# A rewritten attention stage for one transformer trunk, with weight splits and the first map's scaling on POOL

## The chip, the cores and the metric

The kernel runs on one core of one Trainium2 chip. The metric is the device time of one execution in microseconds (us), as the median of the runs; lower is better. Engines: PE is TensorE (matmul), PEld its weight loads, DVE is VectorE, ACT is ScalarE, POOL is GpSimd, SP is SyncE, which here only starts DMAs.

## What is computed

Two residual layers over 512 tokens of width 1024, all in float32. Layer 0 mixes tokens by a gated MLP, layer 1 by differential attention; each is followed by a gated feed-forward block with a width-3 convolution, and each residual sum by a layer norm. The change touches the attention alone:

```
q, k, v = split(x @ w_qkv)           # 8 heads; q, k: 2 maps x 64; v: 128
logits  = q_j . k_j / 8 + bias(head, key - query)      # j = 0, 1
attn    = softmax(logits_0) - lam * softmax(logits_1)
o       = attn @ v                   # 512 x 128 per head
o       = o * rsqrt(mean(o^2) + eps) * subln_g * (1 - lambda_init)
out     = concat(o) @ w_out
```

## The kernel before

Each float32 product is made of three fast matmuls: an operand is split into hi (rounded, by an ACT copy) and lo (the rest, by a subtraction), and PE adds hi·hi, hi·lo and lo·hi in one PSUM bank (product, lines 988 to 994; every 128-wide product has these three lines, whatever the tensor). Tokens lie in four blocks t of 128.

The weights come in units of 128x2048 floats (1 MB). SP loads a unit into w_raw (two buffers), ACT makes w_hi (line 336 or 556), DVE makes w_lo (line 602), PE uses it. The semaphores are w_landed, w_hi_done, w_lo_done and w_used (a count of units that PE has left). Each engine has one instruction stream, written out by hand, and every wait blocks what is behind it on that engine.

The attention stage uses 12 units: U_BV to U_BV+3 for the values (4 heads in each pair of units, 512 columns wide), eight units U_QK+h with the queries and keys of head h, and then four units U_BO for the output product. On PE (lines 1235 to 1353) it runs so: tokens_first makes the values of heads 0 to 3 while the last rows are still being normalised; tokens_group (line 1045) makes those of heads 4 to 7 from U_BV+2 and U_BV+3; project (line 1240) makes q and k of heads 0 and 1 in banks 0 and 1; scores(0) makes the logits of head 0, block by block, in banks 2 (j=0) and 3 (j=1). Then head(h) runs for h = 0 to 6: turn_probs (line 1273) transposes the finished map of head h in 16 pieces through banks 5 and 6; scores (line 1258) makes the logits of head h+1; values (line 1289) multiplies the map by v into bank 7; project makes q and k of head h+2; mean_square (line 1303, matmul on line 1308) sums the squares into bank 4. After head 6 comes head 7 alone, woven with output units 0 and 1. Units 2 and 3 follow in outward (line 1079).

For one head and one block t the softmax is: DVE adds the bias and takes the maximum (scored, line 901, once per j, out of banks 2 and 3), ACT takes the exponential with its row sum (exps, line 525), DVE takes the reciprocals (909), scales the first map (911), makes the factor of the second (913) and mixes the two (917). DVE does scored(t+1) ahead of mixed(t). ACT and DVE split the transposed map (534, 931); ACT copies v_tok, splits each head's v (515, with 888 on DVE), squares the output of a head (541), and takes Ln and Exp for the root (547, 551), each behind a table load of its own. DVE writes the normalised o_t (939). In a head, ACT runs all of exps(h+1), the next unit's w_hi, and only then squares(h); DVE runs all of the softmax of h+1 and then w_lo of the next unit.

The bias tiles (256 KB for each block and head) are loaded by POOL (1471 to 1477) into bias_sb, each when DVE has read the one before. Apart from those, POOL does only the power for the layer norm's root (1465).

## Time and profile before

| | |
|---|---|
| three runs | 1385.53, 1384.03, 1385.91 us; median 1385.53 |
| profiled execution, first to last instruction | 1384.8 us, 15759 instructions |
| PE busy | 1310.7 us (95%) |
| DVE, ACT, POOL busy | 676.2, 460.4, 64.5 us (49%, 33%, 5%) |
| attention, from PE's last value matmul of heads 0 to 3 to its first of output unit 2 | 718.3 to 978.2 us |

Only the span of the profiled execution is given, not a separate time of its own; it lies 0.7 us under the median of the three runs. Matmuls are pipelined: a matmul's own duration is longer than the distance from one start to the next, and the distance is what counts. An entry "x8" or "x2" stands for so many instructions run together. "[1.78 <-ACT o_sq L541]" says that the engine sat idle for 1.78 us and that ACT's line 541 ended it.

### The profile page before, as it was taken

The numbers are of one execution on the slowest core, as the hardware profiler recorded it, in microseconds if no ns is written. First come the engines' busy times: TensorE is split into PE (matmuls) and PEld (weight loads), VectorE is DVE, ScalarE is ACT, GpSimd is POOL, SyncE is SP. The second block draws the span as 40 slices with busy tenths as digits, with TensorE's granted clock in tenths as the row PEclk, the third lists the DMA queues.
The fourth block names the chain that finished last, engine by engine and source line by source line (L and its number), as shares of the span: only waits on it lengthen the run. The fifth ranks groups of instructions, "written<-read, shape, count | busy, mean of one in ns | idle before, by whom it ended". The sixth has DMA issues, their size and how long they took to land.

```text
span 1384.8 us, 15759 instructions
## 1 busy us (share of the span) xinstructions
PE 1310.7 (95%) x6046; PEld 1070.9 (77%) x6046; DVE 676.2 (49%) x875; ACT 460.4 (33%) x549; POOL 64.5 (5%) x82
## 2 busy tenths in 40 slices
PE   7999999998999999999989889897999999999996
PEld 5788887888888888888868566665788888888884
DVE  2537664347433443323652677775664333443227
ACT  2422232213323232223222476765233223232220
POOL 3002000001000000000010100000010000000001
PEclk9999998999999999999999899998999999999998
DMA  7236931231322223223233232221222322223221
GB/s 287 91 92 143 237 107 61 91 122 62 120 92 91 91 91 111 102 91 121 87 98 95 79 99 76 81 87 61 73 80 92 119 93 91 91 91 110 103 91 61
DMA packets 96487, 140.54 MB, mean 101 GB/s; under 512 B 5120, under 2 KB 74840, under 8 KB 96192
## 3 DMA queue, kind: packets, MB, share of 16 engines
q1 hardware_dynamic: 88608, 119.55, 26.5%
q0 software_dynamic: 7840, 20.46, 5.3%
q8 instruction: 26, 0.43, 0.1%
q14 instruction: 13, 0.11, 0.0%
HBM read 137.85 MB, written 10.52 MB: 107 GB/s over the span
## 4 chain that ended last, share of the span: by engine, by line
PE 79%; DVE 10%; ACT 3%; DMA 3%; issue 3%; POOL 1%; DVEq 0%; POOLq 0%; SPq 0%; ACTq 0%
PE bank L990 27%; PE bank L994 25%; PE bank L993 25%; DMA w_raw<-in_a_w_in_dram 3%; DVE w_lo L602 2%; DVE x_tok L626 1%; ACT w_hi L336 1%; DVE r_stat L630 1%; POOL r_rs L1465 1%; DVE x_tok L646 1%; DVE prob L901 1%; PE bank L1308 1%; DVE xt_lo L608 1%; PE bank L1283 1%; DVE s_lo L616 1%
## 5 line engine op out<-in xcount | busy, mean ns | idle before, releaser
L990 PE MATMUL bank<-xt_hi,w_hi 128*128 128x512 f32 (+1 forms) x1024 | 391.2, 382 | 8.1 <-DVE xt_lo L608 6.6
L994 PE MATMUL bank<-xt_hi,w_lo 128*128 128x512 f32 (+1 forms) x1024 | 386.3, 377 | 0.0
L993 PE MATMUL bank<-xt_lo,w_hi 128*128 128x512 f32 (+1 forms) x1024 | 386.3, 377 | 0.0
L602 DVE TENSOR_TENSOR w_lo<-w_raw,w_hi 128x2048 fp32r<-128x2048 f32 x106 | 242.6, 2289 | 292.4 <-ACT w_hi L336 266.1
L990 PEld LDWEIGHTS bank<-xt_hi,w_hi 128*128 128x128 f32 x1024 | 194.1, 190 | 49.7 <-issue 10.3
L336 ACT CAST w_hi<-w_raw 128x2048 fp32r<-128x2048 f32 x60 | 114.5, 1909 | 323.9 <-PE bank L990 271.6
L993 PEld LDWEIGHTS bank<-xt_lo,w_hi 128*128 128x128 f32 x1024 | 194.1, 190 | 35.7 <-issue 1.4
L994 PEld LDWEIGHTS bank<-xt_hi,w_lo 128*128 128x128 f32 x1024 | 194.0, 189 | 35.4
L990 PE MATMUL bank<-w_hi,s_hi 128*128 128x512 f32 x544 | 214.9, 395 | 5.4 <-DVE s_lo L616 5.4
L993 PE MATMUL bank<-w_lo,s_hi 128*128 128x512 f32 x544 | 213.1, 392 | 0.0
L994 PE MATMUL bank<-w_hi,s_lo 128*128 128x512 f32 x544 | 212.9, 391 | 0.0
L990 PEld LDWEIGHTS bank<-w_hi,s_hi 128*128 128x128 f32 x544 | 103.1, 189 | 28.9 <-issue 7.8
L476 ACT CAST w_hi<-w_raw 128x2048 fp32r<-128x2048 f32 x42 | 80.0, 1906 | 134.3 <-PE bank L990 134.3
L993 PEld LDWEIGHTS bank<-w_lo,s_hi 128*128 128x128 f32 x544 | 103.2, 190 | 21.4 <-issue 0.2
L994 PEld LDWEIGHTS bank<-w_hi,s_lo 128*128 128x128 f32 x544 | 103.0, 189 | 21.6
L836 DVE SCALAR_TENSOR_TENSOR conv<-bank,conv_p,conv 128x511 f32<-128x511 f32 x44 | 33.0, 750 | 149.8 <-ACT conv L463 149.8
L463 ACT ACTIVATE conv<-bank,conv_p 128x512 f32<-128x512 f32 x44 | 34.3, 780 | 178.5 <-PE bank L994 178.5
L990 PE MATMUL bank<-w_hi,xt_hi 128*128 128x512 f32 x192 | 77.9, 406 | 13.3 <-DVE w_lo L602 10.9
L853 DVE TENSOR_TENSOR act<-conv,bank 128x512 f32 (+1 forms) x44 | 30.2, 687 | 98.8 <-PE bank L994 98.8
L994 PE MATMUL bank<-w_hi,xt_lo 128*128 128x512 f32 x192 | 76.5, 399 | 0.0
L993 PE MATMUL bank<-w_lo,xt_hi 128*128 128x512 f32 x192 | 76.5, 399 | 0.0
L1465 POOL TENSOR_TENSOR r_rs<-r_ve,neg_half 128x1 f32<-128x1 f32 x16 | 27.3, 1706 | 1011.4 <-DVE r_ve L634 1011.4
(132 smaller groups left out, 1134.4 us busy)
## 6 DMA issues: line engine op xcount, KB each, us to landing
w_raw<-in_f_w_in_dram SPq DMA_DIRECT2D x44, 1024.0 KB, 5.1
w_raw<-in_f_w_down_dram SPq DMA_DIRECT2D x22, 1024.0 KB, 4.8
w_raw<-in_a_w_in_dram SPq DMA_DIRECT2D x16, 1024.0 KB, 5.6
bias_by_query_key<-bias_by_distance POOLq DMA_DIRECT2D x4, 2048.0 KB, 35.9
w_raw<-in_a_w_out_dram SPq DMA_DIRECT2D x8, 1024.0 KB, 4.9
bias_sb<-bias_by_query_key POOLq DMA_DIRECT2D x32, 256.0 KB, 2.9
w_raw<-in_b_w_qkv_dram SPq DMA_DIRECT2D x16, 512.0 KB, 4.9
w_raw<-in_b_w_qkv_dram SPq DMA_DIRECT2D x4, 1024.0 KB, 5.1
```

The costliest lines, as they stand in the source:

```text
L336: act_e.copy(w_hi[:, u % 2, :], w_raw[:, u % 2, :]).then_inc(w_hi_done, 1)
L463: act_e.activation(conv[:, j, :], bank[j][:, :], ACT.Identity, bias=conv_col(l, NCP - 1, off + j), scale=conv_col(l, 1, off + j)).then_inc ...
L476: act_e.copy(w_hi[:, u % 2, :], w_raw[:, u % 2, :]).then_inc(w_hi_done, 1)
L602: dve.tensor_tensor(w_lo[:, u % 2, :], w_raw[:, u % 2, :], w_hi[:, u % 2, :], ALU.subtract).then_inc(w_lo_done, 1)
L608: ins = dve.tensor_tensor(xt_lo[:, 4 * h:4 * h + 4, t * P:t * P + P], bank[2 * t + h][:, :].rearrange("p (k n) -> p k n", n=P), xt_hi[:, 4 ...
L616: dve.tensor_tensor(s_lo[:, k % 2, :, :], src[:, bass.ds(i * (2 * step) + 2 * k, 2), :] if step else src[:, 2 * k:2 * k + 2, :], s_hi[:, k ...
L836: dve.scalar_tensor_tensor(out=conv[:, j, 1:S], in0=bank[j][:, 0:S - 1], scalar=conv_p[:, l, bass.ds(off + j, 1)], in1=conv[:, j, 1:S], op ...
L853: dve.tensor_tensor(dst, conv[:, j, :], bank[2 + j][:, :], ALU.mult).then_inc(act_done, 1)
L990: ins = pe.matmul(o, a_hi, b_hi, start=start, stop=False)
L993: pe.matmul(o, a_hi, b_lo, start=False, stop=False)
L994: return pe.matmul(o, a_lo, b_hi, start=False, stop=stop)
L1465: pool.tensor_tensor(r_rs[:, t:t + 1], r_ve[:, t:t + 1], neg_half[:, 0:1], ALU.pow).then_inc(rstd_done, 1)
```

## The change

The stage keeps its arithmetic and gets a new order on every engine, with all head loops written out.

- Units: the values of heads 4 and 5 (U_V45) and of heads 6 and 7 (U_V67) are units of their own, 256 columns wide, and value_pair multiplies them. U_V45 is woven between the blocks of scores(0), U_V67 between the blocks of the last scores. Project(1) follows scores(0).
- The values are split once, straight out of PSUM (values_hi, values_lo), for all heads; the per-head copies go.
- Within a head PE runs project(h+2) in pieces of 2, 3, 3 and 3, 5 rows of k between transposes, scores and values. mean_square sits behind 9 of the matmuls of project(h+2, 1).
- ACT makes the next unit's w_hi between the transposed pieces, squares(h) ahead of exps(h+1, 3), and loads the Ln table before it waits for the mean square.
- POOL makes w_lo of U_QK0 to U_BO+2 (11 units, four subtractions of 512 columns each), and scales the first map (shares) in place of DVE's line 911. DVE's mixed(t) waits for POOL's shares(t).
- SP loads the bias tiles, in line with the weight units. bias_sb moves to the place of ln_bc.
- Head 7, output units 0 and 1: cut into token blocks and halves. U_BO+2 is split into the place of the values of heads 0 to 3.

```diff
+    U_QK0 = U_BV + 2
+    U_V45 = U_BV + 3
+    U_QK1 = U_BV + 4
+    U_V67 = U_QK1 + H - 1
+    U_BO = U_V67 + 1
...
+        def hi_of(u):
+            if u == U_BO + 2:
+                return val_hi[:, 0:H // 2, :, :].rearrange("p h t n -> p (h t n)")
+            return w_hi[:, u % 2, :]
...
+                if n == 2:
+                    sp.wait_ge(sc_done, 2 * TB * H)
...
+            def load_bias(h):
+                for t in range(TB):
+                    if h:
+                        sp.wait_ge(sc_done, 2 * TB * (h - 1) + 2 * t + 2)
+                    sp.dma_start(bias_sb[:, t, :], bias_dram[h, t * P:t * P + P, :]).then_inc(bias_landed[t], 16)
+
+            load_qk(0)
+            load_unit(U_V45, cols(b_w_qkv[0], 2 * D + NB, 2 * P), dst=raw(U_V45, 2 * P))
+            sp.wait_ge(bias_made, 1)
+            sp.wait_ge(rows_ready, TB * 2)
+            load_bias(0)
+            load_qk(1)
+            load_qk(2)
+            for h in range(1, H - 2):
+                load_bias(h)
+                load_qk(h + 2)
+            load_bias(H - 2)
+            load_unit(U_V67, cols(b_w_qkv[0], 2 * D + NB + 2 * P, 2 * P), dst=raw(U_V67, 2 * P))
+            load_bias(H - 1)
...
+                if u == U_BO + 2:
+                    act_e.wait_ge(pv_mm, H // 2)
...
+                    act_e.wait_ge(ms_mm, h)
...
+            def root(h):
+
+                act_e.preload_act_table_set("natural_log")
+                act_e.wait_ge(ms_mm, h + 1)
...
+                act_e.activation(o_rs[:, :], bank[4][:, :], ACT.Ln, bias=eps_col[:, 0:1]).then_inc(ln_done, 1)
+                act_e.wait_ge(ln_done, h + 1)
+                act_e.activation(o_rs[:, :], o_rs[:, :], ACT.Exp, scale=-0.5).then_inc(rs_o_done, 1)
...
+            weights(U_QK0)
+            for n in range(TB):
+                values_hi(n)
+            weights(U_V45)
+            query_key(0, 0)
+            query_key(0, 1)
+            weights(U_QK1)
+            exps(0, 0)
+            values_hi(TB)
+            exps(0, 1)
+            exps(0, 2)
+            values_hi(TB + 1)
+            exps(0, 3)
+            weights(U_QK1 + 1)
+            query_key(1, 0)
+            query_key(1, 1)
+            for h in range(H - 2):
+                probs_hi(h, 0)
+                probs_hi(h, 1)
+                weights(U_QK1 + h + 2)
+                probs_hi(h, 2)
+                probs_hi(h, 3)
+                exps(h + 1, 0)
+                exps(h + 1, 1)
+                query_key(h + 2, 0)
+                exps(h + 1, 2)
+                squares(h)
+                exps(h + 1, 3)
+                root(h)
+                query_key(h + 2, 1)
+            h = H - 2
+            probs_hi(h, 0)
+            probs_hi(h, 1)
+            weights(U_BO)
+            probs_hi(h, 2)
+            probs_hi(h, 3)
+            exps(h + 1, 0)
+            values_hi(TB + 2)
+            exps(h + 1, 1)
             stationary(o_t, None, 0, o_done, 2)
+            exps(h + 1, 2)
+            values_hi(TB + 3)
+            exps(h + 1, 3)
             weights(U_BO + 1)
+            squares(h)
             stationary(o_t, None, 1, o_done, 4)
-            head(H - 1)
-            outward(o_t, U_BO, U_F[1] - U_BO, o_done, H, begun=True)
+            root(h)
+            h = H - 1
+            probs_hi(h, 0)
+            probs_hi(h, 1)
+            probs_hi(h, 2)
+            probs_hi(h, 3)
+            weights(U_BO + 2)
+            squares(h)
+            root(h)
+            stationary(o_t, U_BO + 1, 2, o_done, 6)
+            weights(U_BO + 3)
+            stationary(o_t, U_BO + 2, 3, o_done, H)
+            weights(U_F[1])
             enter(3, U_F[1])
             ffn(1)
...
+            def weighed(h, t):
+
                 n = TB * h + t
-                dve.wait_ge(exp_done, 2 * n + 2 + (0 if i is None else i * (4 * TB)))
+                dve.wait_ge(exp_done, 2 * n + 2)
                 dve.reciprocal(rsum[:, t, :], psums[:, t, :]).then_inc(rs_done, 1)
-                dve.wait_ge(rs_done, n + 1 + dyn4)
-                dve.tensor_scalar(prob[:, t, 0, :], prob[:, t, 0, :], rsum[:, t, 0:1], None, ALU.mult
-                                  ).then_inc(p0_done, 1)
+                dve.wait_ge(rs_done, n + 1)
                 dve.tensor_scalar(c1[:, t:t + 1], rsum[:, t, 1:2], neg_lam[:, 0:1], None, ALU.mult
                                   ).then_inc(c1_done, 1)
-                dve.wait_ge(p0_done, n + 1 + dyn4)
-                dve.wait_ge(c1_done, n + 1 + dyn4)
+
+            def mixed(h, t):
+
+                n = TB * h + t
+                dve.wait_ge(p0_done, n + 1)
+                dve.wait_ge(c1_done, n + 1)
                 dve.scalar_tensor_tensor(out=prob[:, t, 0, :], in0=prob[:, t, 1, :], scalar=c1[:, t:t + 1],
                                          in1=prob[:, t, 0, :], op0=ALU.mult, op1=ALU.add).then_inc(mixp_done, 1)
...
+            for n in range(TB):
+                values_lo(n)
+            query_key(0, 0)
+            query_key(0, 1)
+            scored(0, 0)
+            weighed(0, 0)
+            values_lo(TB)
+            scored(0, 1)
+            mixed(0, 0)
+            weighed(0, 1)
+            scored(0, 2)
+            mixed(0, 1)
+            weighed(0, 2)
+            values_lo(TB + 1)
+            scored(0, 3)
+            mixed(0, 2)
+            weighed(0, 3)
+            mixed(0, 3)
+            query_key(1, 0)
+            for h in range(H - 2):
+                query_key(h + 1, 1)
+                probs_lo(h, 0)
+                probs_lo(h, 1)
+                scored(h + 1, 0)
+                probs_lo(h, 2)
+                probs_lo(h, 3)
+                weighed(h + 1, 0)
+                scored(h + 1, 1)
+                mixed(h + 1, 0)
+                weighed(h + 1, 1)
+                query_key(h + 2, 0)
+                scored(h + 1, 2)
+                mixed(h + 1, 1)
+                weighed(h + 1, 2)
+                scored(h + 1, 3)
+                mixed(h + 1, 2)
+                weighed(h + 1, 3)
+                mixed(h + 1, 3)
+                values(h)
...
+            def value_pair(u, b, t, frees=0):
+
+                if t == 0:
+                    unit_ready(u)
+                    if u == U_V45:
+                        pe.wait_ge(xt_lo_done, TB * 3)
+                    else:
+                        pe.wait_ge(qk_lo_done, 2 * H)
+                hi = w_hi[:, u % 2, :].rearrange("p (k n) -> p k n", n=2 * P)
+                lo = w_lo[:, u % 2, :].rearrange("p (k n) -> p k n", n=2 * P)
+                for k in range(KD):
+                    ins = product(bank[b + t // 2][:, t % 2 * 2 * P:t % 2 * 2 * P + 2 * P], xt_hi[:, k, t * P:t * P + P],
+                                  xt_lo[:, k, t * P:t * P + P], hi[:, k, :], lo[:, k, :], k == 0, k == KD - 1,
+                                  frees if k == 0 else 0)
+                if t % 2:
+                    ins.then_inc(bv_mm, 1)
...
+            project(0, 0, range(KD), 1)
+            project(0, 1, range(KD))
+            for t in range(TB):
+                value_pair(U_V45, 4, t, 1 if t == 0 else 0)
+                scores(0, t)
+            project(1, 0, range(KD), 1)
+            project(1, 1, range(KD))
+            for h in range(H - 2):
+                turn_probs(h, 0, 1)
+                turn_probs(h, 1)
+                project(h + 2, 0, range(0, 2))
+                turn_probs(h, 2)
+                scores(h + 1, 0)
+                turn_probs(h, 3)
+                project(h + 2, 0, range(2, 5))
+                scores(h + 1, 1)
+                values(h, 0)
+                project(h + 2, 0, range(5, KD))
+                scores(h + 1, 2)
+                values(h, 1)
+                values(h, 2)
+                scores(h + 1, 3)
+                values(h, 3)
+                project(h + 2, 1, range(0, 3))
+                mean_square(h)
+                project(h + 2, 1, range(3, KD))
+            h = H - 2
+            turn_probs(h, 0, 1)
+            turn_probs(h, 1)
+            value_pair(U_V67, 0, 0)
+            turn_probs(h, 2)
+            scores(h + 1, 0)
+            turn_probs(h, 3)
+            value_pair(U_V67, 0, 1)
+            scores(h + 1, 1)
+            value_pair(U_V67, 0, 2)
+            scores(h + 1, 2)
+            value_pair(U_V67, 0, 3)
+            scores(h + 1, 3)
+            for k in range(TB):
+                values(h, k)
             out_ready(U_BO, S_BO, 0)
-            out_unit(U_BO, 0, (0, 1), start=True)
-            turn_probs(H - 1, (2, 3))
-            values(H - 1, range(TB))
-            mean_square(H - 1)
-
+            pe.wait_ge(bv_lo_done, TB + 4)
+            out_unit(U_BO, 0, (0,), start=True, frees=1)
+            mean_square(h)
+            h = H - 1
+            turn_probs(h, 0)
+            turn_probs(h, 1)
+            pe.wait_ge(sc_done, 2 * TB * H)
+            out_unit(U_BO, 0, (1,), start=True)
+            turn_probs(h, 2)
+            turn_probs(h, 3)
+            values(h, 0)
+            values(h, 1)
             out_ready(U_BO, S_BO, 1)
-            out_unit(U_BO, 1, (0, 1))
+            out_unit(U_BO, 1, (0,))
+            values(h, 2)
+            values(h, 3)
+            out_unit(U_BO, 1, (1,))
+            mean_square(h)
+            pe.wait_ge(at_lo_done, TB * H)
+            out_unit(U_BO, 0, (2,), start=True, halves=(1,))
+            out_unit(U_BO, 0, (3,), start=True, halves=(0,))
+            out_unit(U_BO, 1, (2,), halves=(1,))
+            out_unit(U_BO, 1, (3,), halves=(0,))
+            pe.wait_ge(ln_done, H)
+            out_unit(U_BO, 0, (2,), start=True, halves=(0,))
             pe.wait_ge(o_done, H)
-            out_unit(U_BO, 0, (2, 3), start=True)
-            out_unit(U_BO, 1, (2, 3), frees=1)
+            out_unit(U_BO, 0, (3,), start=True, halves=(1,))
+            out_unit(U_BO, 1, (2,), frees=1, halves=(0,))
+            out_unit(U_BO, 1, (3,), halves=(1,))
             outward(U_BO, U_F[1] - U_BO, S_BO, 3, first=2)
...
+            def weights(u):
+
+                pool.wait_ge(w_hi_done, u + 1)
+                pool.wait_ge(w_lo_done, u)
+                for c in range(4):
+                    part = slice(c * NB, c * NB + NB)
+                    ins = pool.tensor_tensor(lo_of(u)[:, part], w_raw[:, u % 2, part], hi_of(u)[:, part], ALU.subtract)
+                ins.then_inc(w_lo_done, 1)
+
+            def shares(h, t):
+
+                pool.wait_ge(rs_done, TB * h + t + 1)
+                pool.tensor_scalar(prob[:, t, 0, :], prob[:, t, 0, :], rsum[:, t, 0:1], 1.0, ALU.mult, ALU.mult
+                                   ).then_inc(p0_done, 1)
+
+            weights(U_QK0)
+            weights(U_V45)
+            weights(U_QK1)
             for t in range(TB):
-                pool.dma_start(bias_sb[:, t, :], bias_dram[0, t * P:t * P + P, :]).then_inc(bias_landed[t], 16)
-            with pool.Fori(1, H) as h:
+                shares(0, t)
+            weights(U_QK1 + 1)
+            for h in range(1, H):
+                weights(U_QK1 + h + 1)
                 for t in range(TB):
-
-                    pool.wait_ge(sc_done, (h - 1) * (2 * TB) + (2 * t + 2))
-                    src = bias_dram[bass.ds(h, 1), t * P:t * P + P, :].rearrange("a p k -> p (a k)")
-                    pool.dma_start(bias_sb[:, t, :], src).then_inc(bias_landed[t], 16)
+                    shares(h, t)
+            weights(U_BO + 1)
+            weights(U_BO + 2)
+
```

## Rows read from the trace of the kernel before

**Rows 1.** Stages of the attention part, core 0: us, then busy us (x instructions) of each engine, TensorE clock, DMA share, GB/s

```profile
767.00:782.00 15.00, 9.54 (x32) 5.64 (x32) 12.53 (x35) 8.24 (x19) 2.19 (x4) 0.63 0.23 70
...
830.90:855.00 24.10, 21.94 (x102) 15.73 (x102) 17.80 (x41) 15.56 (x30) 2.19 (x4) 1.00 0.32 87
...
928.50:949.00 20.50, 12.59 (x55) 7.97 (x52) 15.32 (x39) 14.52 (x26) 0.00 (x0) 0.82 0.00 0
```

**Rows 2.** Who waited for whom, the whole run: total us, times, longest

```profile
PE bank L1308 <- ACT o_sq L541: 14.5, 8, 3.1
```

**Rows 3.** PE in order of time, head 3: start us, us, instruction, idle before

```profile
829.25 1.04 PE L1283 MATMUL bank<-ident,prob 128*128 128x128 f32 x8
...
837.58 0.58 PE L990 MATMUL bank<-qk_hi 64*128 64x512 f32 x2
...
838.55 0.50 PE L990 MATMUL bank<-xt_hi,w_hi 128*128 128x512 f32 x1
838.89 0.40 PE L993 MATMUL bank<-xt_lo,w_hi 128*128 128x512 f32 x1
...
847.24 1.13 PE L1308 MATMUL bank<-o_sq,ones 128*128 128x512 f32 x2 [1.78 <-ACT o_sq L541]
...
850.97 0.39 PE L990 MATMUL bank<-xt_hi,w_hi 128*128 128x512 f32 x1
...
853.46 0.39 PE L994 MATMUL bank<-xt_hi,w_lo 128*128 128x512 f32 x1
853.70 1.03 PE L1283 MATMUL bank<-ident,prob 128*128 128x128 f32 x8
```

**Rows 4.** PE in order of time, the edges of the attention part

```profile
718.26 0.39 PE L994 MATMUL bank<-w_hi,xt_lo 128*128 128x512 f32 x1
720.70 0.47 PE L990 MATMUL bank<-w_hi,xt_hi 128*128 128x512 f32 x1 [2.05 <-DVE w_lo L602]
...
779.38 1.33 PE L1283 MATMUL bank<-ident,prob 128*128 128x128 f32 x5 [1.10 <-DVE prob L917]
...
978.17 0.47 PE L990 MATMUL bank<-w_hi,s_hi 128*128 128x512 f32 x1 [0.40 <-DVE s_lo L616]
```

**Rows 5.** PE in order of time, 256-column matmuls of the first feed-forward block

```profile
325.07 0.28 PE L990 MATMUL bank<-xt_hi,w_hi 128*128 128x256 f32 x1
...
327.47 0.28 PE L994 MATMUL bank<-xt_hi,w_lo 128*128 128x256 f32 x1
```

**Rows 6.** Instruction groups of DVE and ACT, whole run: busy us, mean ns, idle before

```profile
L602 DVE TENSOR_TENSOR w_lo<-w_raw,w_hi 128x2048 fp32r<-128x2048 f32 x106 | 242.6, 2289 | 292.4 <-ACT w_hi L336 266.1 <-ACT w_hi L476 26.3
...
L901 DVE CUSTOM_DVE_ANT_0 prob<-bank,bias_sb 128x512 f32<-128x512 f32 x64 | 41.5, 686 | 8.4 <-PE bank L994 8.4
...
L917 DVE SCALAR_TENSOR_TENSOR prob<-prob,c 128x512 f32<-128x512 f32 x32 | 24.0, 751 | 3.4
...
L534 ACT CAST at_hi<-bank 128x512 fp32r<-128x512 f32 x32 | 17.3, 589 | 19.6 <-PE bank L1283 19.6
...
L547 ACT ACT_TABLE_LOAD x8 | 10.3, 1283 | 0.1
```

**Rows 7.** POOL in order of time, start of the run and one layer-norm step

```profile
1.47 0.29 POOL L1408 TENSOR_SCALAR_AFFINE_SELECT ident<-ident 128x128 f32<-128x128 f32 x1
1.73 0.97 POOL L1410 IOTA dist_row<- 32x1024 f32 x1
...
677.46 1.51 POOL L1465 TENSOR_TENSOR r_rs<-r_ve,neg_half 128x1 f32<-128x1 f32 x1 [345.69 <-DVE r_ve L634]
```

**Rows 8.** PE and TensorE clock around an earlier stop: us, PE busy, clock, DMA share, GB/s

```profile
694.00:696.00 2.00, 0.14 (x1) 0.96 0.00 0
696.00:698.00 2.00, 2.00 (x5) 0.50 0.32 65
698.00:700.00 2.00, 2.00 (x7) 0.69 1.05 408
```

**Rows 9.** DMA issues in the window 690 to 1000 us: KB each, median us to landing

```profile
w_raw<-in_b_w_qkv_dram SPq DMA_DIRECT2D x16, 512.0 KB, 4.9
```

More of the change, by code:

```diff
@@ L77, in encoder_kernel @@
     U_END = U_D[1] + FB * D // UC
[L78 removed]
+    N_AV, N_AU = U_AU - U_AV, U_AO - U_AU
     frev = nc.dram_tensor("bias_by_distance", (H, SPAN), F32).ap()
@@ L322, in landed_count @@
             same = [v for v in range(u % 2, u + 1, 2)]
-            return 16 * sum(2 if U_QK <= v < U_BO else 1 for v in same)
+            return 16 * sum(2 if v == U_QK0 or U_QK1 <= v < U_V67 else 1 for v in same)
         @block.scalar
@@ L519, in exps @@
-            def exps(h, i=None):
-                dyn = 0 if i is None else i * (4 * TB)
-                for t in range(TB):
-                    for j in range(2):
-                        act_e.wait_ge(sc_done, 2 * TB * h + 2 * t + j + 1 + dyn)
-                        act_e.activation(prob[:, t, j, :], prob[:, t, j, :], ACT.Exp, bias=nmax[:, t, j:j + 1],
-                                         scale=-1.0, accum_out=psums[:, t, j:j + 1]).then_inc(exp_done, 1)
-            def probs_hi(h, i=None):
-                dyn = 0 if i is None else i * (2 * TB)
-                for k in range(TB):
-                    act_e.wait_ge(at_mm, TB * h + k + 1 + dyn)
-                    if k == 0 and h >= 1:
-                        act_e.wait_ge(pv_mm, h + (0 if i is None else i * 2))
-                    act_e.copy(at_hi[:, k, :], bank[5 + k % 2][:, :]).then_inc(at_hi_done, 1)
@@ L581, in _, with exps @@
-            with act_e.Fori(0, H // 2 - 2) as i:
-                for j in range(2):
-                    head(j, i, lambda: qk_weights(U_QK + j + 3, i))
-            head(H - 4, None, lambda: weights(U_QK + H - 1))
-            head(H - 3, None, lambda: weights(U_BO))
-            head(H - 2)
+            def exps(h, t):
+                for j in range(2):
+                    act_e.wait_ge(sc_done, 2 * TB * h + 2 * t + j + 1)
+                    act_e.activation(prob[:, t, j, :], prob[:, t, j, :], ACT.Exp, bias=nmax[:, t, j:j + 1],
+                                     scale=-1.0, accum_out=psums[:, t, j:j + 1]).then_inc(exp_done, 1)
@@ new lines, in _ @@
+            h = H - 2
+            query_key(h + 1, 1)
+            probs_lo(h, 0)
+            probs_lo(h, 1)
+            scored(h + 1, 0)
+            probs_lo(h, 2)
+            probs_lo(h, 3)
+            weighed(h + 1, 0)
+            values_lo(TB + 2)
+            scored(h + 1, 1)
+            mixed(h + 1, 0)
+            weighed(h + 1, 1)
+            scored(h + 1, 2)
+            stationary(o_t, S_BO, 0)
+            mixed(h + 1, 1)
+            weighed(h + 1, 2)
+            values_lo(TB + 3)
@@ L974, in _ @@
+            scored(h + 1, 3)
+            mixed(h + 1, 2)
+            weighed(h + 1, 3)
+            mixed(h + 1, 3)
+            stationary(o_t, S_BO + 1, 1)
+            values(h)
+            h = H - 1
+            for k in range(TB):
+                probs_lo(h, k)
+            values(h)
+            stationary(o_t, S_BO + 2, 2)
+            weights(U_BO + 3)
+            stationary(o_t, S_BO + 3, 3)
             enter(3, U_F[1])
```

370 lines of the change are left out of this document (133 added, 237 removed).

## Prediction

> **What bounds the kernel now.** Read the engines' shares first: PE is busy for 95% of the span, so a change pays only where PE stands still or runs at half clock. Then the stages. Most of the kernel leaves nothing to gain, but the attention stage does. [rows 1] show three of its stretches: 15 us around the first softmax with 9.5 us of PE work at a clock of 0.63, 24.1 us of a middle head with 21.9, and 20.5 us at head 6 with 12.6. DVE is busy for 17.8 of the 24.1 us, so it isn't full; it is in the wrong order. The waits say which order: the mean square waits for ACT's square eight times, 14.5 us in all [rows 2], because ACT puts four pairs of exponentials and a weight unit ahead of it. The largest other waits are at the first softmax and before the output product. The stage's ends are in [rows 4]: PE stops at 718.3, restarts at 720.7, begins the transposes of head 0 at 779.4, and begins output unit 2 at 978.2.
>
> **Prices.** From [rows 3]: a 128x512 matmul starts 0.227 us after the one before (12 in a row, 850.97 to 853.46); the first after a switch costs 0.34, so a switch is 0.11. A block of scores, six matmuls with j=0 and j=1 side by side, takes 0.97 (837.58 to 838.55). Eight transposes take some 0.85 (1.04 with the pipeline's end), the mean square 1.2. A 256-column matmul comes every 0.120 us (20 steps in 2.40) [rows 5]: 24 of them are a value block of 2.9, and cutting half of the values in this way costs 192 x 0.120 against 96 x 0.227, or 1.2 us more PE work. From [rows 6]: DVE's score step is 0.62 from start to start (0.686 less the overlap), its mix 0.68, its split of a unit 2.29, ACT's copy of a transposed piece 0.59, a table load 1.28.
>
> POOL's subtraction and its scaling are in no row. Lower end: the iota writes a column in 0.95 ns, so 512 columns take 0.5 us [rows 7]. Upper end: one column of TENSOR_TENSOR (a power) takes 1.51, and the affine select, which reads and writes 128 columns, takes 0.29, four times that is 1.16; together 2.7. The affine select is the nearest row, a plain pass over one input. For the scaling I take 0.85, between 0.5 and its 1.16; for the subtraction, with a second input but the fixed part paid once instead of four times, 1.2, or 4.8 a unit against DVE's 2.29. The Trainium skill speaks against this move (GPSIMD Engine Reference, Engine selection): elementwise work with two inputs belongs on VectorE, GpSimd being some 2 times slower. Its table gives 4.5 us for 2048 columns; by it the sum below would be 0.3 us shorter at the restart and the same elsewhere. No row here shows it.
>
> **Step 1, the start.** ACT makes w_hi of U_QK0 when it made U_BV+2's, so POOL can start its split at 718.3, where DVE starts today; it ends at 723.1 in place of 720.6. PE stands still for 4.8 us instead of 2.4, and after such a stop the clock falls: a stop of 2 to 3 us earlier in this trace is followed by 3 us at 0.50 to 0.69 [rows 8], which costs some 1.6. Then project(0) 11.1, four value blocks 11.9, four score blocks 3.9, project(1) 11.1. The transposes of head 0 begin at 723.2 + 1.6 + 38.0 = 762.8, not 779.4. The softmax of head 0 is covered by value blocks (each t has 3.9 us; DVE needs 2.8) and its last block by project(1). That is 16.6 us gained, though 11.5 of it is value work that now comes later.
>
> **Step 2, six middle heads.** Today one takes 24.45 (829.25 to 853.70 [rows 3]). New PE work: 60 matmuls 13.6, eight switches 0.9, transposes in three lots 1.85, scores 3 x 0.97 and one of 1.5 (its second bank is late), mean square 1.2: 21.9 to 22.0. Does anything make PE wait? I followed each engine from the head's first transpose, at 0. ACT: query_key, two pieces, then the unit's w_hi from 1.9 to 3.8, two more pieces, exps(0) from 5.3. DVE: at_lo(0) ready at 2.2, and the transpose that needs it comes at 2.3 (a near tie). POOL: w_lo of the unit from 3.9 to 8.7, and only then shares(0) to 9.5, though its input is there at 7.3. DVE reaches mixed(0) at 8.8, so it waits 0.8; then weighed(1), and query_key's q, which can't be split before 11.2 anyway. The late share is absorbed there. scored(2) runs 11.9 to 13.1, scores(3) come at 12.8, the last mix ends at 19.2, and the next head's transposes want it at 22.0: 2.8 us of slack. The square is ready at 15.9 for a mean square at 17.2; Ln starts at 18.7, after a table load already paid, and the square-root's Exp ends at 21.3, before query_key's k at 22.2. So nothing but near ties: 6 x (24.45 - 21.95) = 15 us gained. DVE loses w_lo, the v split and the scaling (some 5 us a head), ACT its v copy: none of it counts, because neither bounds the head. The bias tiles leave POOL's queue for SP's, ahead of the weight unit in order: SP waits for the fourth scored (15.9), issues, and the unit lands after 4.9 [rows 9], near 21.7, where ACT wants it at 23.9 (1.9 of the next head). 2.2 us of slack, so no cost.
>
> **Step 3, the tail.** Today 51.7 from head 6's first transpose (779.4 + 6 x 24.5) to output unit 2. New: transposes of two heads 3.8, V67 11.9, scores 3.9, values 2.9 and 3.0, output units 0 and 1 22.5 with their switches, mean squares 2.4, and waits: 0.8 for query_key of head 7, 0.3 for the square, 1.6 for ACT's root before it can copy head 7's pieces. 53.1: a loss of 1.4, although 11.9 of work was added. From unit 2 on nothing differs; its successor's weights again wait for unit 2 to start.
>
> **Sum.** 16.6 + 15 - 1.4 = 30. For the near ties (a few tenths for seven heads) I take off 1.5: 28.5, to 1356.3 on the span of 1384.8. The span stands 0.7 below the median of the runs, so the forecast is **1357.0**.
>
> **Rivals.** (a) *POOL's splits come late.* shares(0) waits in POOL's queue behind four subtractions. The slack is used up when 3.9 + 4w + s passes 10.4, with s the scaling: at w = 1.4. Past that each head loses the excess. At w = 2.0, s = 0.9 it is 2.3 a head, 14 for six, and 3.2 at the start: 1374. For it: the power's 1.51 on a single column. Against: a pow is no subtraction.
> (b) *The same, and slower than before.* Every us of w costs 4 x 6 + 4 = 28. The gain of 28.5 is gone where w passes 2.5; at 2.7, the upper end, the loss a head is 5.2, 31 for six and 6 at the start, so 1394. Only the highest bound reaches it.
> (c) *DVE and POOL in each other's way.* If each DVE mix stood behind one POOL instruction of 1.2, two mixes ahead of scores(3) would push them by 2.4, less 0.5 of slack: 1.9 a head, some 13 in all, 1370. Against: the order lets POOL scale t+1 only after mixed(t). The Trainium skill has this rule (SBUF — State Buffer, Who interferes with whom): a DVE instruction with two SBUF inputs and a POOL instruction that reads SBUF exclude each other for their whole length. No row shows it.
> (d) *Nothing to measure*: the saved waits come back elsewhere, in SP's longer queue above all. If each unit landed 5.5 us later than I reckon, 3.3 past the slack would stay in each of six heads, 20, and as much again as two heads at the edges: 27 of the 28.5 gone, about 1384.
>
> **Chances.** The forecast's own case, 1350 to 1364: 0.61. Cases (a) and (c): 0.21. (b): 0.09. (d): 0.05. Better than 1350 (the clock stays up, POOL is quick): 0.04. A measurement of this kernel can tell 0.2%, 2.8 us, from no change. Faster 0.86, same 0.05, slower 0.09. The range goes from 1350 to 1376, which leaves out (b), (d) and the far ends.
>
> **What would show it.** Right: transposes of head 0 near 763, heads of 22 us, the mean square's wait gone from [rows 2], unit 2 near 948 to 950, POOL's subtraction at 1.0 to 1.4, DVE waiting under 1 us for the first share of a head. Wrong: PE waiting for nmax or prob in every head with POOL busy just before (a, b); DVE mixes or POOL scalings much longer than their shortest ones (c); ACT's w_hi waiting for the DMA (d). If the stop at 718 is followed by a full clock, step 1 is 1.6 better.

## The result and the profile after

The changed kernel takes **1345.84 us** (median of 4 runs, 1345.01 to 1347.53) against 1385.36 for the kernel before in the same measurement (4 runs, 1384.03 to 1385.91): ratio 0.9721, interval 0.9707 to 0.9734, 39.5 us faster. The forecast said 1357.0 with a range of 1350 to 1376. The sign was right; the time lies 11.2 us below the forecast and 4.2 us below the range.

The page of the changed kernel, engines' busy time:

```profile
span 1343.3 us, 15635 instructions
...
PE 1296.3 (96%) x6142; PEld 1067.0 (79%) x6142; DVE 635.7 (47%) x830; ACT 456.6 (34%) x541; POOL 135.9 (10%) x135
```

POOL has gone from 64.5 to 135.9 us, DVE from 676.2 to 635.7, and PE's share of the span has barely moved. What shrank is the time in which PE did nothing or worked at half clock. The stage windows that answer to [rows 1] (softmax of head 0, a middle head, head 6; columns as there):

```profile
740.00:755.00 15.00, 15.00 (x93) 12.43 (x92) 9.28 (x25) 7.72 (x16) 5.15 (x7) 1.00 0.38 111
781.00:802.00 21.00, 21.00 (x104) 15.22 (x103) 13.74 (x35) 15.52 (x30) 7.81 (x8) 1.00 0.36 101
888.00:908.50 20.50, 20.50 (x143) 17.48 (x142) 12.85 (x33) 11.79 (x23) 7.82 (x8) 1.00 0.13 52
```

PE was at work for 9.5 of 15 us at a clock of 0.63, for 21.9 of 24.1, and for 12.6 of 20.5 at 0.82 [rows 1]. In these three windows it is now never idle and the clock is full. PE's waits between 690 and 970 us (total us, times, longest):

```profile
PE bank L1062 <- POOL w_lo L1591: 4.6, 1, 4.6
PE bank L1062 <- DVE w_lo L649: 3.0, 1, 3.0
PE bank L1366 <- DVE at_lo L968: 1.5, 1, 1.5
...
PE bank L1062 <- DVE qk_lo L936: 0.6, 1, 0.6
```

The mean square's eight waits for ACT's square, 14.5 us in [rows 2], are gone. The single stops left are these four, 0.8 for xt_lo, and one of 0.3 for s_lo, and none lies between the transposes of head 0 and of head 6. PE in order of time, at the edges of [rows 4] and of a middle head (head 1):

```profile
715.06 0.39 PE L1066 MATMUL bank<-w_hi,xt_lo 128*128 128x512 f32 x1
720.08 0.77 PE L1062 MATMUL bank<-xt_hi,w_hi 128*128 128x512 f32 x1 [4.63 <-POOL w_lo L1591]
...
759.34 0.49 PE L1366 MATMUL bank<-ident,prob 128*128 128x128 f32 x3
...
780.29 1.03 PE L1366 MATMUL bank<-ident,prob 128*128 128x128 f32 x8
...
792.96 0.71 PE L1062 MATMUL bank<-qk_hi 64*128 64x512 f32 x2
...
794.06 0.50 PE L1062 MATMUL bank<-at_hi,val_hi 128*128 128x512 f32 x1
...
796.96 1.02 PE L1390 MATMUL bank<-o_sq,ones 128*128 128x512 f32 x2
797.41 0.80 PE L1062 MATMUL bank<-xt_hi,w_hi 128*128 128x512 f32 x1
...
801.27 1.03 PE L1366 MATMUL bank<-ident,prob 128*128 128x128 f32 x8
...
885.20 0.38 PE L1366 MATMUL bank<-ident,prob 128*128 128x128 f32 x2
...
936.90 0.47 PE L1062 MATMUL bank<-val_hi,s_hi 128*128 128x512 f32 x1
```

Head 6's first transpose in the kernel before:

```profile
926.52 1.04 PE L1283 MATMUL bank<-ident,prob 128*128 128x128 f32 x8
```

From these rows and those of before [rows 4], the 41.5 us between the two spans (1384.8 and 1343.3) come apart so:

| stretch | before | after | gain | forecast |
|---|---|---|---|---|
| up to PE's last value matmul of heads 0 to 3 | 718.3 | 715.1 | 3.2 | 0 |
| from there to head 0's transposes | 61.1 | 44.3 | 16.8 | 16.6 |
| six heads | 147.1 | 125.9 | 21.3 | 15 |
| head 6's transposes to output unit 2 | 51.7 | 51.7 | 0.0 | -1.4 |
| output unit 2 to the end | 406.6 | 406.4 | 0.2 | 0 |
| allowance for near ties | | | | -1.5 |

The first line is not the change's. The transposes of x_tok ("the turn of x_tok" below), upstream of every edit, begin at 703.0 and 701.6 in two executions of the kernel before and at 699.95 in the variant of it with only its square moved, at 699.8 and 700.6 in two executions of the changed kernel, and at 699.9 to 701.7 in variants of that. This point varies by 3 us between executions, whatever the kernel. The second line depends on the execution too: in the second trace of the kernel before, the same stretch took 62.8 us (716.85 to 779.60) in place of 61.1, because the clock fell behind the same stop.

POOL and DVE in order of time, first unit and head 1:

```profile
715.03 4.95 POOL L1591 TENSOR_TENSOR w_lo<-w_raw,w_hi 128x512 fp32r<-128x512 f32 x4 [15.44 <-ACT w_hi L372]
...
783.94 5.04 POOL L1591 TENSOR_TENSOR w_lo<-w_raw,w_hi 128x512 fp32r<-128x512 f32 x4 [6.82 <-ACT w_hi L372]
788.95 0.72 POOL L1597 TENSOR_SCALAR prob<-prob,rsum 128x512 f32<-128x512 f32 x1
790.62 0.70 POOL L1597 TENSOR_SCALAR prob<-prob,rsum 128x512 f32<-128x512 f32 x1 [0.95 <-DVE rsum L953]
```

```profile
789.70 0.75 DVE L963 SCALAR_TENSOR_TENSOR prob<-prob,c 128x512 f32<-128x512 f32 x1 [0.66 <-POOL prob L1597]
798.10 0.75 DVE L963 SCALAR_TENSOR_TENSOR prob<-prob,c 128x512 f32<-128x512 f32 x1 [0.57 <-POOL prob L1597]
```

The two prices that no row of before showed are now there: a subtraction of 512 columns 1.26 us (5.04 for four), taken as 1.2; a scaling 0.70, taken as 0.85. The first mix of the head starts 9.4 us after its transposes (forecast 9.5) and waits 0.66 for the share (forecast 0.8).

### The profile page after: what moved, and what is told of

The parts are those of the page before. It is cut to its first block, busy times and chain, and to the rows that moved or that the text cites. A ratio compares the mean times of both kernels' runs of the same rounds, so it can differ in the third digit from the quotient of the medians.

```text
span 1343.3 us, 15635 instructions
## 1 busy us (share of the span) xinstructions
PE 1296.3 (96%) x6142; PEld 1067.0 (79%) x6142; DVE 635.7 (47%) x830; ACT 456.6 (34%) x541; POOL 135.9 (10%) x135
## 4 chain that ended last, share of the span: by engine, by line
PE 88%; DVE 7%; POOL 2%; ACT 1%; issue 1%; DMA 0%; POOLq 0%; DVEq 0%; ACTq 0%
PE bank L1062 29%; PE bank L1065 28%; PE bank L1066 28%; DVE w_lo L649 2%; DVE x_tok L673 1%; DVE r_stat L677 1%; POOL r_rs L1579 1%; DVE x_tok L693 1%; PE bank L1366 1%; DVE xt_lo L655 1%; ACT w_hi L372 1%; PE bank L1076 1%; PE bank L1390 0%; POOL w_lo L1591 0%; DVE s_lo L663 0%
## 5 line engine op out<-in xcount | busy, mean ns | idle before, releaser
L649 DVE TENSOR_TENSOR w_lo<-w_raw,w_hi 128x2048 fp32r<-128x2048 f32 x93 | 212.8, 2289 | 246.4 <-ACT w_hi L372 220.0
L372 ACT CAST w_hi<-w_raw 128x2048 fp32r<-128x2048 f32 x63 | 120.4, 1912 | 299.6 <-PE bank L1062 254.0
L1062 PE MATMUL bank<-w_hi,s_hi 128*128 128x512 f32 x528 | 207.9, 394 | 1.5 <-DVE s_lo L663 1.5
L1066 PE MATMUL bank<-w_hi,s_lo 128*128 128x512 f32 x528 | 206.2, 391 | 0.0
L1065 PE MATMUL bank<-w_lo,s_hi 128*128 128x512 f32 x528 | 206.2, 391 | 0.0
L512 ACT CAST w_hi<-w_raw 128x2048 fp32r<-128x2048 f32 x42 | 80.1, 1907 | 134.4 <-PE bank L1062 134.4
L1066 PEld LDWEIGHTS bank<-w_hi,s_lo 128*128 128x128 f32 x528 | 99.6, 189 | 21.0
L1065 PEld LDWEIGHTS bank<-w_lo,s_hi 128*128 128x128 f32 x528 | 99.7, 189 | 20.4 <-issue 0.2
L1062 PE MATMUL bank<-w_hi,xt_hi 128*128 128x512 f32 (+1 forms) x224 | 83.5, 373 | 11.4 <-DVE w_lo L649 8.3
L1065 PE MATMUL bank<-w_lo,xt_hi 128*128 128x512 f32 (+1 forms) x224 | 81.6, 364 | 0.0
L1066 PE MATMUL bank<-w_hi,xt_lo 128*128 128x512 f32 (+1 forms) x224 | 81.4, 363 | 0.0
```

What stands on the lines that cost most here:

```text
L372: act_e.copy(hi_of(u), w_raw[:, u % 2, :]).then_inc(w_hi_done, 1)
L512: act_e.copy(w_hi[:, u % 2, :], w_raw[:, u % 2, :]).then_inc(w_hi_done, 1)
L649: dve.tensor_tensor(w_lo[:, u % 2, :], w_raw[:, u % 2, :], w_hi[:, u % 2, :], ALU.subtract).then_inc(w_lo_done, 1)
L1062: ins = pe.matmul(o, a_hi, b_hi, start=start, stop=False)
L1065: pe.matmul(o, a_hi, b_lo, start=False, stop=False)
L1066: return pe.matmul(o, a_lo, b_hi, start=False, stop=stop)
```

## The experiments

Eleven runs in three batches; each ratio is against runs of the kernel before on the same chip (medians 1383.94, 1385.34, 1383.98). The theory: the new order of the work brings the gain, and POOL must only not be late. The first rival: POOL's relief of DVE is part of the gain. The second: the mean square's wait was most of it, and the rest of the rewriting little. Beside them stand the questions where the start loses time, and from which lateness of POOL the gain is gone.

**The changed kernel once more**, as the reference of the first batch.

> The changed kernel once more, with nothing changed. In the first pair of profiles PE's last value matmul of heads 0 to 3 came at 715.0 us against 718.3 before, though nothing upstream of it differs in the code. If that is the luck of one execution, this profile puts it somewhere between 715 and 719 and the time differs by as much; if it comes from the change, it is again near 715. The middle heads should again take 21.0 us each.

1346.49 us (1345.67 to 1347.08, 5 runs), ratio 0.9723 (0.9706 to 0.974). It repeats the first result.

**The scaling back on DVE.**

```diff
                 dve.wait_ge(rs_done, n + 1)
+                dve.tensor_scalar(prob[:, t, 0, :], prob[:, t, 0, :], rsum[:, t, 0:1], None, ALU.mult
+                                  ).then_inc(p0_done, 1)
...
-                for t in range(TB):
-                    shares(h, t)
```

> The scaling of the first map goes back to DVE (0.49 us each), POOL keeps the weight splits. Theory (the order on PE makes the gain, DVE has room): the heads stay at 21.0 us, because DVE's two waits for POOL (0.66 and 0.57 us a head) go as the four scalings (some 0.4 each in its stream) come; the time is the same within 2 us of the changed kernel. Rival (what POOL takes from DVE makes the gain): DVE is late again, heads of 22.6 us or more, at least 10 us slower.

1345.97 us (1344.69 to 1347.94, 5 runs), ratio 0.9723 (0.9704 to 0.9741): no difference. Its window of the same middle head:

```profile
781.00:802.00 21.00, 21.00 (x104) 15.21 (x102) 15.40 (x40) 15.49 (x28) 5.23 (x4) 1.00 0.37 102
```

DVE is busy for 15.4 us instead of 13.7, POOL for 5.2 instead of 7.8, and PE for all 21.00 in both. Where the first map is scaled does not matter to this kernel's time.

**The first query-key unit split by DVE**, all else as in the changed kernel.

```diff
+            weights(U_QK0)
             for n in range(TB):
                 values_lo(n)
...
-            weights(U_QK0)
             weights(U_V45)
```

> Only the unit U_QK0, for which PE stands still, is split by DVE in one instruction (2.29 us) ahead of its values_lo; POOL keeps all other units. Theory: PE restarts after about 2.9 us in place of 5.0 (2.3 for the split and 0.6 for values_lo of block 0, which now comes behind it), and the clock stays up or falls for less: 2 to 3.5 us faster than the changed kernel. Rival (the stop is set by the unit's landing or by ACT): no difference.

1343.80 us (1342.33 to 1345.38, 5 runs), ratio 0.9707 (0.9688 to 0.9725): 2.7 us under the changed kernel of the batch. PE's restart, and its clock behind the restart in the changed kernel (us, PE, PEld, DVE, ACT, POOL, clock, DMA share, GB/s):

```profile
718.86 0.47 PE L1063 MATMUL bank<-xt_hi,w_hi 128*128 128x512 f32 x1 [2.65 <-DVE val_lo L918]
```

```profile
716.00:720.00 4.00, 0.00 (x0) 0.00 (x0) 2.02 (x4) 0.90 (x2) 3.98 (x4) 0.98 0.01 2
720.00:722.00 2.00, 1.92 (x5) 1.58 (x6) 0.00 (x0) 1.06 (x1) 0.00 (x0) 0.50 0.33 86
722.00:724.00 2.00, 2.00 (x8) 1.60 (x7) 0.00 (x0) 0.84 (x1) 1.08 (x1) 0.69 1.11 330
```

With POOL, PE stands still for 4.63 us and then works for 3 us at half clock, 1.2 GHz. With DVE the stop is 2.65 us, and the first matmul (0.47 instead of 0.77 us) already runs at 2.4 GHz. From the turn of x_tok to head 0's transposes it is 3.4 us less (56.1 against 59.5): 2.0 of stop, and 1.5 of clock by the rows above. Of the places where POOL's work was moved back to DVE, this is the one where the offload does harm.

**The same again**, as the reference of the third batch.

> The kernel with the split of the first query-key unit on DVE, once more, as the reference point for the next run. From its first measurement (1343.80 us) both theories expect 1342.5 to 1345.5.

1342.73 us (1341.71 to 1344.4, 5 runs), ratio 0.9705 (0.9692 to 0.9718).

**Ten units' splits and the scaling on DVE**; POOL keeps output units 0, 1 and 2. The scaling's line on DVE is that of the run above, and POOL's own calls go; both are left out here.

```diff
             for n in range(TB):
                 values_lo(n)
+            weights(U_V45)
...
             scored(0, 0)
+            weights(U_QK1)
...
             mixed(0, 3)
+            weights(U_QK1 + 1)
...
                 mixed(h + 1, 3)
+                weights(U_QK1 + h + 2)
                 values(h)
```

> The changed kernel with the splits of ten units (the first query-key unit to the values of heads 6 and 7) and the scaling of the first map on DVE; POOL keeps only the splits of output units 0, 1 and 2. In a head DVE makes the next split (2.3 us) behind its last mix. Theory 'the gain is the order, POOL carries nothing that matters': DVE is busy for about 17.5 to 18 of 21 us, PE stays at 21.0 a head, and the time is within 1.5 us of the kernel with only the first split on DVE (1342.3 to 1345.3). Rival 'POOL's relief of DVE is part of the gain': PE waits for mixes, transposed pieces or w_lo in every head, 0.5 us a head or more, and the time is 1347 or more.

1342.27 us (1341.67 to 1343.66, 5 runs), ratio 0.9698 (0.9685 to 0.9711), the same as its reference within the spread. A middle head, and the split in it:

```profile
781.00:802.00 21.00, 21.00 (x106) 15.19 (x103) 17.44 (x40) 15.49 (x29) 0.00 (x0) 1.00 0.38 101
```

```profile
796.32 2.28 DVE L649 TENSOR_TENSOR w_lo<-w_raw,w_hi 128x2048 fp32r<-128x2048 f32 x1
```

With POOL idle, DVE works 17.4 of 21 us, no more than its 17.8 of 24.1 before [rows 1], and PE waits for nothing. **The gain is that of the new order of the work, not of the engine that does it**; the first rival falls. The order has many parts, and only the square's place was tried by itself (below): what the single splitting of the values, the bias tiles on SP's queue or the pieces of project give is not shown, nor is what POOL's three output units give. The split fits behind the head's last mix, where DVE has nothing else to do. This kernel and the one ahead of it are the fastest of the study.

**ACT's square behind the last exponentials.**

```diff
                 exps(h + 1, 2)
-                squares(h)
                 exps(h + 1, 3)
+                squares(h)
                 root(h)
```

> ACT's order in a middle head: the square comes behind the last pair of exponentials, as it did before, everything else stays. Theory (the place of the square is one of the waits that the change takes away): the square is ready some 1.2 us later, PE waits about 0.7 us for it in each of six heads, 3 to 5 us slower than the changed kernel. Rival (the matmuls of the projection that now stand ahead of the mean square cover it): no difference.

1347.46 us (1347.43 to 1348.55, 5 runs), ratio 0.9731 (0.9714 to 0.9748): 1.0 us over the changed kernel of its batch by the medians. In the trace six heads take 128.2 us against 125.9, so 2.3 us more, 0.4 a head. Both are less than was expected:

```profile
799.81 0.39 PE L1066 MATMUL bank<-xt_hi,w_lo 128*128 128x512 f32 x1
800.33 1.12 PE L1390 MATMUL bank<-o_sq,ones 128*128 128x512 f32 x2
800.89 0.79 PE L1062 MATMUL bank<-xt_hi,w_hi 128*128 128x512 f32 x1
```

The mean square starts 0.52 us after the matmul ahead of it, where 0.23 is the distance without a wait. The nine matmuls placed ahead of it cover most of a later square: of the old wait of 1.78 us only 0.3 comes back.

**The kernel before once more**, a look at where its time varies.

> The kernel before once more, with nothing changed, for its profile. If the 3.2 us upstream of the attention stage are luck, PE's last value matmul of heads 0 to 3 comes between 715 and 719 us; if they belong to this kernel, near 718.3 again.

1386.42 us in one run, span 1384.9. Its transposes of x_tok begin at 701.6, not 703.0, and it loses that lead again behind the stop, where the clock is low for 4 us:

```profile
719.29 0.47 PE L990 MATMUL bank<-w_hi,xt_hi 128*128 128x512 f32 x1 [2.05 <-DVE w_lo L602]
```

```profile
720.00:724.00 4.00, 4.00 (x13) 3.12 (x12) 2.21 (x1) 1.75 (x1) 0.00 (x0) 0.60 0.82 231
```

**The kernel before with only its square moved** ahead of the unit's w_hi.

```diff
                 if h + 1 < H:
                     exps(h + 1, i)
+                squares(h, i)
                 if next_unit is not None:
                     next_unit()
-                squares(h, i)
```

> The kernel before with one call moved: ACT squares a head's output ahead of the next unit's weight copy in place of behind it. Theory (PE's wait for the square is bound by ACT's order): the square is 1.8 us earlier, the wait of 1.8 us a head falls to about 0.3, six heads, some 9 us faster than before. Rival (another wait takes its place at the head's start): less than 3 us.

1377.09 us (1375.08 to 1379.2, 4 runs), ratio 0.9944 (0.9927 to 0.996): 8.3 us, as expected. PE's waits in the stage (total us, times, longest):

```profile
PE bank L990 <- DVE qk_lo L880: 4.5, 6, 0.9
...
PE bank L1308 <- ACT o_sq L541: 3.4, 2, 2.7
```

Of the 14.5 us of mean-square waits [rows 2] 11.1 go, and the wait of project for qk_lo grows from 3.5 to 4.5. A head takes 22.8 us instead of 24.5 (800.01 to 822.79), against 21.0 in the changed kernel. One moved line gives a fifth of the whole gain; the second rival falls, as far as the wait can be taken out of the old order.

**POOL made slower, in three sizes.** POOL makes one, two or four of a unit's four subtractions twice; the result is unchanged, the unit is ready 1.26, 2.5 or 5 us later. The edit for two:

```diff
+                for c in range(2):
+                    part = slice(c * NB, c * NB + NB)
+                    ins = pool.tensor_tensor(lo_of(u)[:, part], w_raw[:, u % 2, part], hi_of(u)[:, part], ALU.subtract)
+                ins.then_inc(again, 1)
+                passes.append(u)
+                pool.wait_ge(again, len(passes))
                 for c in range(4):
```

> One of the four subtractions of each of the 11 units is made twice on POOL, 1.25 us more a unit. Where is the edge of the slack? By the prediction's sum shares(0) ends at 3.9 + 5 x 1.25 + 0.7 = 10.85, 0.45 past the 10.4 at which the slack was used up: PE waits a few tenths in each head, too short for the clock to fall, heads of 21.2 to 21.5, and with 1.25 more at the first stop the time is 1349 to 1351. Rival 'every stop costs clock, however short': heads of 22.5 or more, 1357 or more. Third: PE waits for nothing in the heads (the six-subtraction kernel lost its time only past a later edge): 1347 to 1348.5.

> The changed kernel with six subtractions of 512 columns in place of four in every unit that POOL splits (the first two are done twice), 2.5 us more a unit. Theory (a head has about 0.95 us of room for a late first share: 0.44 until DVE's query_key and 0.5 until the last scores): 1.5 us more in each of six heads and 2.5 at the start, some 12 us slower than the changed kernel. Rival (POOL's time is covered all through the heads): 2.5 us slower.

> The same with eight subtractions, each done twice, 5.0 us more a unit. Theory: 4.1 us in each of six heads and 5 at the start, some 30 us slower than the changed kernel, three quarters of the gain gone. Rival: 5 us slower.

| subtractions a unit | us (runs) | ratio (interval) | us a head in the trace, mean of six |
|---|---|---|---|
| 4 | 1345.84 (4) | 0.9721 (0.9707 to 0.9734) | 21.0 |
| 5 | 1353.22 (4) | 0.978 (0.9765 to 0.9795) | 21.8 |
| 6 | 1369.85 (4) | 0.9891 (0.9875 to 0.9908) | 24.1 |
| 8 | 1393.52 (4) | 1.006 (1.0043 to 1.0076) | 27.4 |

All three lose more than was expected. What a head loses is read from the blocks of scores(3), first with five subtractions, then with six (head 1):

```profile
797.49 0.49 PE L1062 MATMUL bank<-qk_hi 64*128 64x512 f32 x1 [0.36 <-DVE nmax L946]
...
798.10 0.49 PE L1062 MATMUL bank<-qk_hi 64*128 64x512 f32 x1
...
798.99 0.50 PE L1062 MATMUL bank<-at_hi,val_hi 128*128 128x512 f32 x1
```

```profile
800.09 0.50 PE L1062 MATMUL bank<-qk_hi 64*128 64x512 f32 x1 [1.55 <-DVE nmax L946]
```

```profile
785.74:810.34 24.60, 23.05 (x103) 16.58 (x102) 14.07 (x36) 15.49 (x28) 10.34 (x10) 0.93 0.31 87
789.00:801.00 12.00, 10.45 (x53) 7.06 (x50) 7.32 (x21) 5.95 (x15) 8.95 (x8) 1.00 0.15 44
801.00:806.00 5.00, 5.00 (x16) 3.68 (x14) 3.26 (x11) 3.88 (x8) 1.39 (x2) 0.66 0.52 146
```

With five, PE waits 0.36 us, and the two score blocks j=0 and j=1 no longer run side by side (x1 and x1 instead of x2): scores(3) takes 1.50 us (797.49 to 798.99) against 1.10 in the changed kernel (792.96 to 794.06). 0.36 + 0.40 is the 0.8 a head. With six, the wait is 1.55, the blocks again 0.4, and the clock falls for the 5 us behind the stop to a mean of 0.66: at a clock of 0.66, 5 us do the work of 3.3, so 1.7 are lost. 1.55 + 0.4 + 1.7 = 3.65, against 24.6 - 21.0 = 3.6. But the clock does not fall in every head. With six subtractions, heads 1, 2, 3 and 5 take 24.5 to 24.6 us, and heads 0 and 4 take 23.0. Head 4 has as long a stop as any, and full clock behind it:

```profile
873.85 0.50 PE L1062 MATMUL bank<-qk_hi 64*128 64x512 f32 x1 [1.62 <-DVE nmax L946]
```

```profile
875.00:880.00 5.00, 5.00 (x21) 3.50 (x20) 3.34 (x11) 3.98 (x9) 1.40 (x2) 1.00 0.57 169
```

1.62 + 0.4 = 2.0 is all that this head loses (23.0 - 21.0). The stops of 0.3 to 0.4 with five subtractions left the clock full in all six heads.

With eight the sequence goes on (nmax 20.5 us in six waits, w_lo 14.7 in three) and the kernel is slower than before, by 0.6%. That is rival (b), reached on purpose: its price is real, and POOL's actual 1.26 us is far from it. It is not far from the edge of rival (a): one more subtraction a unit already costs 0.8 us a head.

## Why the prediction was right and where it was wrong

The step that failed is step 2's sum of PE's work in a middle head: 21.95 us forecast, 20.98 measured, and in it above all the last block of scores, taken at 1.5 us and measured at 1.10. The tail and the allowance erred to the same side, and 3.2 us of chance upstream came on top.

**Step 1, the start: right.** 16.8 us against 16.6, with the stop (4.63 for 4.8) and the half clock behind it both as priced. That loss was accepted as part of the change; the run with DVE's split shows it could be avoided. By the figure of 4.5 us for one two-input instruction of 2048 columns (the Trainium skill, GPSIMD Engine Reference, Elementwise — side-by-side cycle accounting) the split was to be shorter than the 4.95 to 5.04 that its four instructions took. The advice of the Trainium skill (GPSIMD Engine Reference, Engine selection) against two-input work on GpSimd holds here at the one unit that PE waits for, and costs nothing where the split is covered.

**Step 2, the heads: the mechanism right, the PE sum mis-sized.** Every queue behaved as it was followed: the mean square's wait gone, POOL's share 0.1 us from its time, no waits of PE at all, SP's units in time. But a head takes 20.98 us, not 21.95. The terms "scores 3 x 0.97 and one of 1.5 (its second bank is late)" came to 3 x 0.90 and 1.10, 0.6 less in all; the transposes to 1.73 instead of 1.85; the mean square with its switch to 0.9 (from 796.96 to 801.27 less 15 x 0.227), not 1.3. The other matmuls and switches came to 0.15 more than taken. The 1.5 was a near tie decided against the change. The run with five subtractions measured exactly 1.50 for it, in the case where the second bank comes free 0.6 us after the first block's start; here DVE leaves it 0.15 us after that start (793.11 against 792.96). Six times 0.97 is 5.8 us, half of the miss.

**Step 3, the tail: 1.4 us too dear.** 51.7 as before, not 53.1. The waits named came, smaller together: 0.6 for query_key of head 7, none for the square, 1.5 for head 7's pieces (forecast 0.8, 0.3 and 1.6); the rest, 0.8, was not taken apart; the same rounding up of score blocks and transposes is the likely cause.

**The sum.** The 1.5 us for near ties was taken off although none of the ties went wrong. The time was set 0.7 above the span; the changed kernel's profiled run took 1345.01 with a span of 1343.3, so 1.7 lie around the span. Together, in spans: 6.3 for the heads (5.8 as above; the rest is that six heads before are 147.1, not 6 x 24.45), 1.4 for the tail, 1.5 for the allowance, 3.2 upstream, which is chance, and 0.6 for the start, the end and rounding, 13.0; less 1.0 for what lies around the span and 0.8 from the profiled run to the median: 11.2.

**The range.** Its lower end was 1350, and "better than 1350 (the clock stays up, POOL is quick): 0.04". The cases it named did not happen: the clock fell, and POOL was a little slower than taken. What happened stood in no case: all small PE prices were taken from their dear side, an allowance came on top, and the one execution of before was the latest of the three at the turn of x_tok. The forecast's own case should have reached down by the sum of these, to some 1345.

**The rivals.** (a) and (b) had their edge in the right place: "3.9 + 4w + s passes 10.4". With five subtractions the left side is 3.9 + 6.3 + 0.7 = 10.9, an excess of 0.5, and PE waits 0.36; with six it is 12.2, an excess of 1.8, and PE waits 1.55. With the scaling at 0.70 the edge lies at w = 1.45, and the subtraction takes 1.26. What failed is "past that each head loses the excess": with five a head loses 0.8, with six 2.0, or 3.6 where the clock falls. The two score banks fall apart, 0.4, and a fallen clock adds 1.7. From four subtractions to eight, w goes from 1.26 to 2.52; by the two rivals' rule the heads were to lose 6 x (3.9 + 10.1 + 0.7 - 10.4) = 26 us and the start 5, together 31, and the time rose by 47.7. The forecast of 1394 at w = 2.7 comes close to the 1393.5 measured at an effective 2.5 because two errors cancel: a gain 11 us too small, and a price a third too low.
(c) was not seen, but its mechanism is in the rows, and the prediction's "No row shows it" was wrong. The order never puts a mix beside a POOL instruction (POOL's 788.95 and 790.62, DVE's mix 789.70 between them), and mixes take 0.749 us on average, 0.751 before [rows 6]. With the scaling on DVE, seven scalings fell beside POOL's split. Here are the longest with the subtraction that it met, another, and one that met none:

```profile
739.91 1.44 DVE L955 TENSOR_SCALAR prob<-prob,rsum 128x512 f32<-128x512 f32 x1
```

```profile
739.77 1.29 POOL L1593 TENSOR_TENSOR w_lo<-w_raw,w_hi 128x512 fp32r<-128x512 f32 x1
```

```profile
788.16 0.64 DVE L955 TENSOR_SCALAR prob<-prob,rsum 128x512 f32<-128x512 f32 x1
...
791.32 0.49 DVE L955 TENSOR_SCALAR prob<-prob,rsum 128x512 f32<-128x512 f32 x1
```

All seven, 0.62 to 1.44 us long, end 0.28 or 0.29 us after the end of the subtraction that they met (741.35 against 741.06 for the first). A scaling that meets a subtraction waits for its end. The rule of exclusion (the Trainium skill, SBUF — State Buffer, Who interferes with whom) names, besides DVE instructions with two inputs, tensor_scalar where it uses both ports, and has the other engine blocked for the whole instruction; the trace agrees. The seven waits cost no time because PE's work covered them. The trace of the kernel before shows the other direction, POOL's power beside a DVE instruction with two SBUF inputs:

```profile
677.30 1.28 DVE L642 SCALAR_TENSOR_TENSOR x_tok<-x_tok,r_mv,ln_bc 128x1024 f32<-128x1024 f32 x1
...
693.52 2.28 DVE L602 TENSOR_TENSOR w_lo<-w_raw,w_hi 128x2048 fp32r<-128x2048 f32 x1
```

```profile
693.68 2.52 POOL L1465 TENSOR_TENSOR r_rs<-r_ve,neg_half 128x1 f32<-128x1 f32 x1 [8.89 <-DVE r_ve L634]
```

The power takes 1.51 us beside the first [rows 7] and 2.52 beside the second, and ends 0.4 us after the DVE instruction both times, as do all sixteen of the run. By this, the 1.51 that the prediction took as POOL's upper price for one column is mostly a wait. Whether a mix would be held up by a subtraction was not tried.
(d) fell: no w_hi in the heads was late, units landed 5.0 us after their issue as before.

## What to carry to other kernels

Where a stage's bound engine is to be busy without a gap, its time is a plain sum of start-to-start distances: take each from a row, decide no tie against the change without a row, and add no allowance on top of the range. Slack worked out from the queues' order finds the edge to 0.3 us, but the price past it is more than the excess: count the overlap that the wait breaks, and as a risk the clock behind the stop. Before crediting an offload to another engine, put the work back in the new order: here DVE had room for all of it, and the slower engine did harm at the one place where the bound engine waits for it. Before taking a price from a row, look at what the other engines did beside it.

## What was not expected of the hardware

- A short stop in the middle of full work can cost more in clock than in time: behind four of the six stops with six subtractions (1.54 to 1.62 us of idle PE) the clock fell, in heads that were otherwise full, in head 1 to a mean of 0.66 over 5 us. Stops of 0.3 to 0.4 us left it at 1.00.
- The same stop does not always do it. 1.62 us cost clock in heads 2 and 5 and none in head 4. At the start of the stage 2.65 us were followed by full clock in three executions of the variants. In the kernel before and its variant with the square moved, 2.05 us were followed by full clock twice (2.00 us of work in 722 to 724 at 1.00 in the first trace [rows 4]) and by 4 us at a mean of 0.60 once, although PE's work from the turn of x_tok to the restart, 17.7 us, is the same to some 0.03 us in the three. What decides stays open.
- Two score blocks on the two halves of the array take 0.90 us when both banks are free, 1.10 when the second is free 0.15 us after the first block's start, and 1.50 when it is free 0.6 us after.
- A DVE scaling of 512 columns that meets a POOL subtraction waits for its end: all seven ended 0.28 or 0.29 us after it, 0.62 to 1.44 us long in place of 0.49. DVE's score step, which reads one input from PSUM, keeps its 0.69 us beside the same subtractions (at 785.37 in the changed kernel).
